# A streaming encoder step on one core: the recurrences' first tile prepared inside the input projection, and level pairs made for half the tokens in three rounds

## What is computed

```python
a = jnp.where(strict, jnp.einsum('bhid,bhjd->bhij', kb, kc) * decay, 0.0)
sol = lax.linalg.triangular_solve(eye + a, rhs, left_side=True, lower=True)
u, wk = sol[..., :dv], sol[..., dv:]
v_new = u - jnp.einsum('bhcd,bhde->bhce', wk, s)
...
diff = b[:, :, :, None, :] - b[:, :, None, :, :]
decay = jnp.exp(jnp.where(causal[:, :, None], diff, -jnp.inf))
a = jnp.einsum('bhid,bhjd,bhijd->bhij', qc, kc, decay)
o = o_inter + jnp.einsum('bhij,bhje->bhie', a, vc)
```

## Time and profile before

| | us |
|---|---|
| median of 3 runs | 3234.21 |
| lowest, highest | 3232.44, 3240.81 |
| the profiled execution's own time | 3232.9 |
| its span | 3231.2 |
| PE busy | 3084.7 (95%) |
| DVE, ACT, POOL busy | 1578.7, 1026.8, 1523.4 |

### The profile page before, as it was taken

How to read it: one execution, slowest core, us unless ns; L and a number is a source line. 1 busy time by engine, 2 the same in 40 slices (tenths; PEclk the granted TensorE clock), 3 DMA queues, 4 the chain that set the end, 5 groups by cost and what they waited for, 6 DMA issues and landing times. The chain is left out here.

```text
span 3231.2 us, 67218 instructions
## 1 busy us (share of the span) xinstructions
PE 3084.7 (95%) x28484; PEld 2894.3 (90%) x28484; DVE 1578.7 (49%) x2179; ACT 1026.8 (32%) x1834; POOL 1523.4 (47%) x1161
## 2 busy tenths in 40 slices
PE   7999977888898999999999999999999999999999
PEld 6988866777798999999999999877699999999998
DVE  5650035655666445554344433466646455543323
ACT  4222132333434332221122422256624332231212
POOL 4452143444125776764364556311126766764362
PEclk8999978999899999999999999999999999999999
DMA  6222133433661332236424343567521332238332
GB/s 208 83 79 98 49 107 103 146 101 103 205 201 53 104 108 79 91 119 247 152 85 152 93 146 124 162 219 235 161 79 58 110 97 96 77 120 303 98 137 82
DMA packets 370792, 409.45 MB, mean 127 GB/s; under 512 B 29016, under 2 KB 303537, under 8 KB 369480
## 3 DMA queue, kind: packets, MB, share of 16 engines
q1 hardware_dynamic: 363656, 380.24, 35.5%
q0 software_dynamic: 6848, 25.04, 2.5%
HBM read 272.71 MB, written 134.60 MB: 126 GB/s over the span
## 5 line engine op out<-in xcount | busy, mean ns | idle before, releaser
L864 PE MATMUL PS<-token_block,w_block 128*128 128x288 f32 x9408 | 1271.0, 297 | 13.5 <-POOL w_block L778 6.5
L864 PEld LDWEIGHTS PS<-token_block,w_block 128*128 128x128 f32 x9408 | 1262.2, 190 | 16.5 <-POOL w_block L778 6.1
L778 POOL TENSOR_TENSOR w_block<-w_pair_raw,w_block 128x512 fp32r<-128x512 f32 x224 | 302.6, 1356 | 167.0 <-ACT w_block L774 132.9
L1259 PE MATMUL PS<-act_slot,w_down_split 128*128 128x384 f32 x1872 | 328.5, 336 | 5.3 <-DMA act_slot<-act_dram 4.2
L1259 PEld LDWEIGHTS PS<-act_slot,w_down_split 128*128 128x128 f32 x1872 | 326.2, 188 | 6.9 <-DMA act_slot<-act_dram 5.2
L778 POOL TENSOR_TENSOR w_block<-w_sum,w_block 128x512 fp32r<-128x512 f32 x168 | 225.8, 1359 | 97.1 <-ACT w_block L774 97.0
L774 ACT CAST w_block<-w_pair_raw 128x512 fp32r<-128x512 f32 x224 | 137.5, 621 | 306.2 <-PE PS L864 268.5
L774 ACT CAST w_block<-w_sum 128x512 fp32r<-128x512 f32 x168 | 99.3, 620 | 366.7 <-POOL w_sum L767 235.6
L1231 PE MATMUL PS<-token_block,w_block 128*128 128x288 f32 x1344 | 180.3, 296 | 2.1 <-issue 2.1
L1231 PEld LDWEIGHTS PS<-token_block,w_block 128*128 128x128 f32 x1344 | 179.4, 189 | 2.9 <-issue 2.5
L762 POOL TENSOR_TENSOR w_sum<-w_pair_raw 128x512 f32<-128x512 f32 x56 | 88.0, 1571 | 163.6 <-DMA w_pair_raw<-in_ffn_w_gu_dram 114.8
(11 more groups left out here) (466 smaller groups left out, 5497.9 us busy)
## 6 DMA issues: line engine op xcount, KB each, us to landing
w_pair_raw<-in_ffn_w_gu_dram SPq DMA_DIRECT2D x88, 512.0 KB, 5.1
act_slot<-act_dram SPq DMA_DIRECT2D x28, 1152.0 KB, 13.3
cache_kT<-kT_dram SPq DMA_DIRECT2D x8, 2048.0 KB, 11.4
cache_v<-in_cache_c_v_dram SPq DMA_DIRECT2D x64, 256.0 KB, 4.9
act_dram<-ffn_act_high SPq DMA_DIRECT2D x28, 576.0 KB, 2.8
act_dram<-ffn_act_low SPq DMA_DIRECT2D x28, 576.0 KB, 3.9
down_source<-down_dram SPq DMA_DIRECT2D x56, 288.0 KB, 4.9
xT<-xT_dram SPq DMA_DIRECT2D x24, 576.0 KB, 12.0
```

Source lines behind the costliest of these rows:

```text
L778: self.nc.gpsimd.tensor_tensor(self.blocks[q][:, 1], self.source(p, q), self.blocks[q][:, 0], ALU.subtract).then_inc(self.low, 1)
L864: m = nc.tensor.matmul(to[:, j], w, x[:, j * HN:(j + 1) * HN], start=(q < 3 and i == 0 and t == 0), stop=(q > 3 and i == 3 and t == 2), sk ...
L1259: m = nc.tensor.matmul(down_banks(u)[:, j], wd[u % 2][:, int(q == 2), k], x[:, int(q == 1), group(j)], start=(k == 0 and q == 0), stop=(k ...
```

## The change

1. `first_tile` holds the preparation of tile 0 with semaphores of its own. `rest_projection` runs it in its last block: SP loads q, k, v and the GLA rows when the third block's products are done; POOL, ACT and DVE do their steps there; PE does one step behind each of the row tiles 1 to 7. The next stage starts at turn 0 and gets these steps as semaphore credits. Memsets and casts of turn -1 are divided among the stages and engines. Tile 0's exponents come behind its first block product.
2. The stage no longer ends with a wait for the stores: SP, ACT and DVE wait for them in the next stage.
3. `gla_q_exps` is made for the 64 upper tokens of each level, `gla_k_exps` for the 64 lower ones (the others stay zero), with one instruction a level on each engine, for the levels a tile needs (seven, in the sample tile four). A level's eight products move 64 columns over 128 stationary ones; four levels fit in PSUM; a prompt tile has three rounds of 4, 2 and 2, the sample tile three of 2, 2 and 1. DVE puts a level in two masked copies of 256 elements.
4. In SP's list tile 1's rows and the first keys come ahead of the states.

```diff
+def first_tile(e, ctx, at_):
...
+    def load(sp):
+        for n in range(3):
+            sp.dma_start(lq[n][:], e.scr["qkv"][r, n * HE:(n + 1) * HE]).then_inc(q_in, 16)
+        sp.dma_start(lk[:], e.scr["rest"][r, 2]).then_inc(k_in, 16)
+    def scale(pool):
...
+        y.then_inc(ug_ready, 1)
...
+        tt_(qn[:], q, wide(e.rn[:, NPT, 0:H], DK), ALU.mult).then_inc(scaled, 1)
+        tt_(kn[:], k, wide(e.rn[:, NPT, H:2 * H], DK), ALU.mult).then_inc(scaled, 1)
+        tt_(kb[:], k, wide(e.rkb[:, NPT], DK), ALU.mult).then_inc(scaled, 1)
+        pool.wait_ge(dec_exp, 1)
+        tt_(dec[:], dec[:], over_heads(c("upto_s")), ALU.mult).then_inc(dec_masked, 1)
...
+    def turn_qk(pe, n):
+        pe.wait_ge(scaled, n + 1)
+        if n:
+            pe.wait_ge(tready, n)
+        else:
+            pe.wait_ge(gla_ready, 1)
+        src = (qn, kn, kb)[n]
+        for m in range(4):
+            x = pe.transpose(PS[:, 3, m * P:(m + 1) * P], src[:, 2 * m:2 * m + 2].rearrange("p h v -> p (h v)"), ident)
+        x.then_inc(turned, 1)
...
+    def a_pairs(pe):
+        pe.wait_ge(tready, 3)
+        pe.wait_ge(dec_exp, 1)
+        gram(kbt, a_mm)
+    def p_pairs(pe):
+        pe.wait_ge(bt_ready, 1)
+        gram(qt, p_mm)
...
+    def factors(dve):
+        v.memset(qts, 0.0).then_inc(zeroed, 1)
+        v.memset(qes, 0.0)
+        v.memset(tt64, 0.0)
...
+        even_read(pool)
+        decays_done(pool)
+        begin.scale(pool)
...
+        eng.wait_ge(mm, 3 * NT)
+        eng.wait_ge(w_low, 16)
...
+            if (b, t) == (3, 0):
+                last_keys = NT + NPT
+                even_read(sp)
+                sp.wait_ge(stored[last_keys % 4], 16 * (last_keys // 4 + 1))
+                begin.load(sp)
...
-        for s in range(4):
-            sp.wait_ge(stored[s], 16 * (len(tiles) // 4))
...
+        def first_step(t):
+            if t == 1:
+                decays_done(pe)
+                begin.sums(pe)
+            if t == 2:
+                begin.turn_gla(pe)
+            if t in (3, 4, 5):
+                begin.turn_qk(pe, t - 3)
+            if t == 6:
+                begin.a_pairs(pe)
+            if t == 7:
+                begin.p_pairs(pe)
...
+                if b == 3:
+                    first_step(t)
...
-    rounds_p, rounds_s = [[0, 1], [2, 3], [4, NL], [5, 6]], [[0, 1], [2], [3], [NL]]
+    rounds_p, rounds_s = [[0, 1, 2, 3], [4, NL], [5, 6]], [[0, 1], [2, 3], [NL]]
+    HALF = P // 2
...
-    ql = sb("gla_q_exps", [P, 2, NL, P])
+    ql = sb("gla_q_exps", [P, NL, 2, P // 2])
...
+    def side(ap, j, upper):
+        return ap.rearrange("p m (n y l) -> p m n y l", y=2, l=LEVELS[j])[:, :, :, int(upper)]
+    def levels(k):
+        return [j for jobs in (rounds_s if sample(k) else rounds_p) for j in jobs if j < NL]
...
-        for n in range(-1, NT + 1):
+        for n in range(NT + 1):
             turn(n if 0 <= n < NT else None, n + 1 if n + 1 < NT else None, n - 1 if n >= 1 else None)
+    def rest_stored(eng):
+        for sem in e.rest_stored:
+            eng.wait_ge(sem, 16 * NT)
...
+        rest_stored(sp)
+        load_qk(1)
+        load_keys(0)
+        load_v(0)
+        load_keys(1)
+        load_keys(2)
...
-            for m in range(2):
-                x = tt_(kl[:, m], ex[:, m, 0:NL], over_heads(gkt[:, k % 2, m], NL), ALU.mult)
+            for j in levels(k):
+                x = tt_(side(kl[:, :, j], j, False), side(ex[:, :, j], j, False), side(gkt[:, k % 2], j, False), ALU.mult)
...
-        spread(0)
+        spread(1)
+        nc.gpsimd.memset(S[:], 0.0)
+        nc.gpsimd.memset(GS[:], 0.0).then_inc(states_zeroed, 1)
+        nc.gpsimd.memset(kl[:], 0.0).then_inc(keys_zeroed, 1)
+        pool.wait_ge(keys_zeroed, 1)
+        level_keys(0)
...
-                        w, q = (gkt[:, k % 2, m], gqt[:, k % 2, m]) if j == NL else (kl[:, m, j], ql[:, m, j])
-                        y = mm(PS[:, 4 + h, x * 256 + m * P:x * 256 + (m + 1) * P], w[rows], q[rows], start=True, stop=True)
+                        w, q = (gkt[:, k % 2, m], gqt[:, k % 2, m]) if j == NL else (kl[:, m, j], ql[:, j, m])
+                        n = P if j == NL else HALF
+                        y = mm(PS[:, 4 + h, x * P + m * n:x * P + (m + 1) * n], w[rows], q[rows], start=True, stop=True)
...
-            pairs(i, 3)
...
+            if i == 0:
+                exponents(0)
...
+            if i == 0:
+                level_exps(0)
...
+            if i == 0:
+                rest_stored(act)
...
+        v.memset(u[:], 0.0)
...
+                elif j == NL:
...
+                else:
+                    s = LEVELS[j]
+                    mask = side(c("up")[:, j * P:(j + 1) * P].rearrange("p (a t) -> p a t", a=1), j, True)
+                    for m in range(2):
+                        y = v.copy_predicated(side(to[:, :, m], j, True), bc(mask, (P, 4, HALF // s, s)),
+                                              src[:, :, m].rearrange("p h (n l) -> p h n l", l=s))
...
-            for m in range(2):
-                y = tt_(ql[:, m], ex[:, m, 0:NL], over_heads(gqt[:, k % 2, m], NL), ALU.mult)
+            for j in levels(k):
+                y = tt_(ql[:, j].rearrange("p m (n l) -> p m n l", l=LEVELS[j]), side(ex[:, :, j], j, True),
+                        side(gqt[:, k % 2], j, True), ALU.mult)
...
+    def first_scaled(pool):
+        for done, times in ((ug_ready, 1), (gs_high, 1), (gs_split, 1), (scaled, 3), (dec_masked, 1), (bv_ready, 1),
+                            (kbe_ready, 1), (kd_ready, 1)):
+            pool.sem_inc(done.sem, times)
```

More of the change, by code:

```diff
@@ L2745, in scalar @@
         nc.scalar.activation(at[:], at[:], ACT.Ln, bias=1.0).then_inc(a_tail, 1)
-        for n in range(NT + 6, len(tiles)):
+        for n in range(NT + 6, 3 * NT):
             evict(n)
+        for t in range(NT):
+            evict(3 * NT + t)
+            if t == 1:
+                begin.decays(act)
+            if t == 2:
+                begin.keep_gla(act)
+            if t in (3, 4, 5):
+                begin.keep_qk(act, t - 3)
+            if t == 7:
+                begin.keep_blocks(act)
     def vector(dve):
@@ L2796, in wait, with recurrences @@
             eng.wait_ge(self.sem, k * self.per + (self.per if n is None else n))
-def recurrences(e, ctx, at_, ahead):
+def recurrences(e, ctx, at_, ahead, first):
     nc, d, PS, ident, c = e.nc, e.d, e.PS, e.ident, e.const
@@ L3614, in keep_qk @@
             dst = (qt[:, (k + 1) % 3], kt[:], kbt[:])[n]
-            if sample(k) and n == 0:
-                act.wait_ge(zeroed, 1)
-                for x in range(2):
-                    copy(of_parity(qts[:, x], x), of_parity(PS[:, 3, :].rearrange("p (m t) -> p m t", m=4), x))
             copy(dst, PS[:, 3, :].rearrange("p (m t) -> p m t", m=4)).then_inc(tready.sem, 1)
@@ L3986, in turn @@
                 pairs_decayed(n)
-            if i is not None:
-                place(i, 3)
-            if n is not None:
                 set_blocks(n)
         each(turn)
-    def nothing(eng):
-        return None
     def rows_stored(eng, t):
@@ L4875, in build_program @@
                                                           for (name, shape, dt), spot in zip(held, spots))
+        e.rest_stored = [e.sem(top, f"rest_out{s}") for s in range(4)]
+        spot = e.place()
+        row = spot + 4 * KT * T
+        high = row + 4 * T + 64
+        rest = high + 8 * KT * T
+        middle_at = middle_places(spot, row, high, high + 4 * KT * T, rest, spots[0], spots[-1])
         with ExitStack() as ctx:
@@ L4892, in build_program @@
                 conv, done = conv_projection(e, both, hT, wraw, ws, rest_raw)
[L4893 to L4894 removed]
+                begin = first_tile(e, both, middle_at)
+                together(e, both, conv, rest_projection(e, both, hT, rest_raw, rows, ws_half, base, done, begin))
         e.xT = e.sb(top, "xT", [P, KT, T])
[L4896 removed]
         e.norm_row = e.sb(top, "norm_row", [P, T])
@@ L4908, in build_program @@
                 out, ahead = mixer_out(e, middle, tuple(ByGroup(x) for x in hT), at_, tok, wts)
-                together(e, middle, recurrences(e, middle, at_, ahead), out)
+                together(e, middle, recurrences(e, middle, at_, ahead, begin.tiles), out)
             with e.stage() as first:
```

253 lines of the change are left out of this document (203 added, 50 removed).

## The result

The changed kernel is slower: a median of 3261.38 us in 12 runs (3245.64 to 3275.42) against 3235.77 for the kernel before in 12 runs beside them, ratio 1.0074, 95% interval 1.0058 to 1.0091. The forecast was 3213.5, faster, with 3230 as the range's upper end. Its own profiled execution has a span of 3261.2 us against 3231.2, 30.0 more, with a granted clock of 0.966 against 0.979.

What follows compares the result with a forecast made beforehand. TensorE was taken as busiest almost throughout, except for 30.9 us of half-idle PE at the start of the recurrences. First part -18.0 and second part -1.5 from 3232.9 gave 3213.4, stated as 3213.5 us, range 3196 to 3230.

Steps and rivals of the forecast that it cites:

- the sum of the turns: Turns 2 to 7: placing and rounds -1.2, factors +2.0, so +0.8 each, together +4.8 us.
- Turns 2 to 7 within 1 us of today's: Sign to look for on PE: each of these turns stays within 1 us of its time before.
- Products (a): Pair products in a prompt tile's turn: half the moved columns take the same time, 1.1 us for 16.
- The bound of 0.55: Pair rounds: 16 products take 0.55 us instead of 1.1 if the moved columns alone count.
- the rival that they pay: Pairs: rounds at 0.55 us and a lock cost of 0.3 instead of 2.0 give about 3197; chance 0.23.
- Placing and rounds (b): Prompt tile's turn: eight placements take 3.7 us, half product +2.1, fourth round's removal -3.3; together -1.2.
- Factors (c): DVE's gla_q_exps in seven instructions alternates with POOL's work, ending later: +2.0 us a turn, bounds -0.3 and +4.7.
- the rival that the lock decides by slow POOL instructions: POOL's level instructions take 1.5 us each and DVE waits for them: +7.1 in six turns, about 3247; chance 0.06.
- First tile: Tile 0's preparation between projection row tiles: no waits, PE share 8.0 us, first block product 20.6 earlier, net -18.0.
- The boundary: Between projection and recurrences, without the wait for stores: 1.1 + 1.2 = 2.3 us remain.
- the +2.6 for turn 0: Tile 0's exponents, moved between first and second block step, cost turn 0 2.6 us.
- Last turn: Turn 8: first round's +2.1 falls into PE's 1.71 us wait for keys, last round goes; -4.2 us.

Runs made afterwards that it cites:

- e4: Changed kernel with twelve more key transpositions ahead of each of PE's two waits in turns 2 to 7: 3229.19 us, ratio 0.9987.
- e1: Changed kernel with the level code of before, so without the pairs of half the tokens: 3226.11 us, ratio 0.9968.
- e5: Changed kernel, DVE's put moved between level instructions, and quarters' copies behind the first of four placed levels: 3210.41 us, ratio 0.9951.
- e3: Changed kernel, DVE's put moved behind the second level instruction, and quarters' copies ahead of the first round's placing: 3228.29 us, ratio 0.9980.
- e2: Kernel of before with the changed level code alone (half the tokens, one instruction a level, three rounds): 3267.18 us, ratio 1.0085.
- e9: Changed kernel with only the quarters' copies moved, behind the first of four placed levels: 3238.11 us, ratio 0.9994.
- e10: Kernel of before with DVE's qs_scaled issued three times instead of once in turns 2 to 7: 3274.32 us, ratio 1.0114.
- e7: Kernel of before with DVE's second gla_q_exps instruction issued again ahead of the put in turns 2 to 7: 3286.43 us, ratio 1.0197.
- e12: e5 with 16 transpositions of the identity added in turn 1, where PE waits for dn_states: 3212.72 us, ratio 0.9915.

## Why the prediction was wrong

- **The step that failed** is the sum of the turns, "turns 2 to 7 each -1.2 + 2.0 = +0.8, together +4.8". It charged each us of PE's wait as one us and took the clock behind it as given. At full clock the term was good: +0.1 a turn in e4. Measured it was +35.3 for six turns, and all but 1 us of that is what the lower level added. The forecast had itself said that the put of level 2 is "waited for by PE for 2 us" and that the half product would start 2.1 later (it is 2.4 in e4), and it had read 0.57 in the earlier trace rows; it used that number for the boundary only, and never asked what its own new waits would do to it. "Turns 2 to 7 within 1 us of today's", its own sign, is where it broke.
- **Products (a):** nearly right. 32 products of half the tokens take 1.94 us at full clock (573.12 to 575.06), 0.97 for 16; before 1.11. The bound of 0.55 is excluded, and with it the rival that they pay in the change as made.
- **Placing and rounds (b):** eight placements took 4.25 for 3.7. The whole of the turn behind the half product shrank by 3.8 where 3.3 was taken.
- **Factors (c):** the put came 1.5 us later, +2.0 was taken. POOL needed 456 ns an instruction, forecast 457, so the rival that the lock decides by slow POOL instructions was wrong too: it had the right sign and the wrong cause. DVE's seven instructions took 4.50 in the turn, where one alone takes 279 ns.
- **First tile:** no step of it waits ahead of the boundary, as forecast, and PE's share of it cost 7.4 us (434.36 - 426.97 in e1) for 8.0. The boundary took 3.55, taken as 2.3. The first block product was 16.0 and 19.9 us earlier in two executions, forecast 20.6. The 3.9 between the two arose ahead of the first step: the products with `w_rest_odd` begin at 283.5 in the change, at 279.6 in e1 and at 279.9 before; why stays open. Of the -18.0, 10 are left in e1: the +2.6 for turn 0 was too small (4 to 9 us, see above). The clock is lower there (0.71 to 0.81, in the kernels without the first part 0.81 to 0.91), which was not tried by itself.
- **Last turn:** the -4.2 never showed, not even in e5 (63.9 us to the mixer's first product, before 63.2). The forecast let the first round's delay fall into a wait "for keys" at 863.32, but the earlier trace rows name no engine for it ("issue"). In e5 PE waits for keys at another place:

```profile
825.91 1.73 PE L3715 MATMUL PS<-consts_f,cache_keys 128*128 128x128 f32 x8 [2.45 <-DMA cache_keys<-in_cache_c_k_dram]
```

The sum with the sizes as measured: -16.0 + 5.4 - 1.0 + 35.3 + 3.8 + 2.5 = +30.0. The loss of turns 0 and 8 is put down to the clock by their windows (0.80 and 0.80, before 0.90 and 0.86) and was not tried by itself.

## What to carry to other kernels

On an engine that is nearly full, a new wait of PE costs its own length and, where the granted clock falls behind it, more again: the eleven waits of 1.7 to 1.9 us in turns 2 to 7 cost 35 us by the clock, some 3 each, beside the 19 that they lasted. So price a wait by asking what the clock column shows behind the nearest wait of that size, and keep what PE waits for at the head of the other engines' queues; two exchanges in DVE's list turned a loss of 0.7% into a gain of 0.5%. When a busy share stays and the number of instructions in it falls, read the clock before anything else.

## What the hardware did that I had not expected

- The granted clock can fall behind waits of 1.3 to 1.9 us among small products, and then stays at the lower level for 7 to 14 us in turns 3 to 7 of the change, while PE works almost without a pause (15.54 of 15.55 us busy at 0.56). The Trainium skill (TensorE: Matmul & The Clock Gate, HAM oscillation) describes a kernel whose clock falls in every round behind PE's wait for data, which it draws as 3 to 5 us. The pattern is this one, with another engine as the cause and with shorter waits, of 1.3 to 1.9 us.
- It isn't certain at a given wait: the same wait of 1.38 us ahead of the fourth round was followed by the lower level in one of six turns before, e3's 1.29 in four of five. The 1.8 at the third block step was followed by it in three of six turns of the change, four of six of e2 and five of six of e9, the 1.7 ahead of the half product in all five of the change. Waits of 2.6 and 3.5 us (e10, e7) were followed by it every time. And it can fall without a wait over 0.5 us, around the round of four levels (e12 above).
- Useless work can pay: 144 transpositions, which made the kernel before 1.0% slower, made the changed kernel 0.9% faster.
